# Modulation weights first, probabilities copied in halves, and no scaling of the residual: three edits to one nested two-block transformer kernel

## The chip, the cores and the metric

The kernel runs on one core of a Trainium2 chip. The metric is the device time of one execution, in microseconds (us), as the median of several runs.

## What is computed

Two blocks follow each other on 256 tokens of width 1024, all in 32-bit floats. The first block has two layers, the second has one and a mixture of experts. Cut to what matters here:

```python
# first block: x (256 x 1024) and a context ctx (256 x 1024), two layers i = 0, 1
shift, scale, gate = split(silu(c) @ w_ada[i] + b_ada[i], 3)          # the "modulation"
u, uc = h * (1 + scale) + shift, hc * (1 + scale_c) + shift_c
y, yc = mixer_a(u, uc, ...) if i == 0 else mixer_b(u, uc, ...)        # attention with a gate, 16 heads of 64
h  = layer_norm(ALPHA * h  + gate   * y,  ln_g[i], ln_b[i])           # ALPHA = 4 ** 0.25
hc = layer_norm(ALPHA * hc + gate_c * yc, ln_g[i], ln_b[i])           # only after layer 0
# layer_norm divides by sqrt(var + 1e-5)
# second block, on the 256 rows of h: modulation, dilated attention beside a depthwise
# convolution of width 31, then 32 experts of hidden width 512, two for each token
```

Layer norm doesn't change when its input is divided by a constant, if its 1e-5 is divided by the square of that constant.

## The kernel before, in words

Activations are held turned: features on the 128 partitions, tokens along the free dimension. `H` holds the residual as 8 tiles of 128 x 512 (256 tokens of x, 256 of ctx). Each engine has its own program; semaphores order them.

**Weights.** All weights of the three layers come as chunks of 1024 x 512 (2 MB, 2048 KB in the profile) through `ring`, which has six slots (`SLOTS`). `PLAN` (line 111) fixes their order: four chunks of `ada0` (the modulation of layer 0), three of `a_in`, two more of `ada0`, and so on. SyncE issues them (lines 367 to 379); from the seventh on it waits until the slot's last user is done. Ahead of that loop it issues a table (`cst`), the rows of x and ctx (lines 364, 365), and then line 366 waits for all small vectors. Behind chunk 4 (the first of `a_in`) it issues two constant tables (lines 378, 379).

**The prologue.** ScalarE's queue issues 13 small loads of vectors, the taps of the convolution (`conv_w`) and the sinks (lines 841 to 849). TensorE waits for all of them but the sinks, turns them (lines 472 to 477), then turns the rows of x and ctx, 32 transposes of 128 x 128 in eight groups, which VectorE copies to `H` (line 1081). Then `modulation` (line 507) goes through the four chunks: `stream` (line 486) multiplies a chunk by silu(c) as soon as it has landed, ScalarE copies the row to SBUF (line 861), and `fold` (line 498) turns it into columns. VectorE makes `mod` from them (lines 1100, 1090) and the modulated input `uT` (lines 1105, 1107). TensorE waits for the two tables (line 552) and then runs `in_proj` of `a_in` (line 539), 22 jobs that leave through four PSUM banks.

**Attention.** `attention` stands three times: L = "a" (16 units with 4 key tiles, called lat, then 16 with 2, called ctx), "b" (16 units with 4 key tiles), "c" (8 units with 1 or 2). A unit is two heads of 128 queries. TensorE, for unit n: turns the probabilities of n (line 593), computes the scores of n + 3 (line 583), waits until ScalarE has copied the turned probabilities to `probT` (line 911, one instruction for all key tiles), multiplies them by the values (line 603). ScalarE, after the copy of n, makes the exponentials of n + 2 (line 896, for "a" also line 900 for the sink). VectorE, in its turn n: takes the output of n - 1 (line 1186 or 1188), adds mask or bias to the scores of n + 3 and reduces them to a maximum (lines 1210 or 1221, 1151 to 1156), then divides the exponentials of n + 2 by their sum (lines 1173, 1177).

**The residual.** After `a_in`, ScalarE multiplies all of `H` by ALPHA in place, eight instructions (line 884), before the first exponential of attention "a". VectorE multiplies `ln_g` and `ln_b` of layer 0 by ALPHA (lines 1279, 1280), so that the output of the first layer norm is scaled too. `residual` (line 1239) waits for both by `alpha_ok` and adds gate * y to `H`.

**The experts.** SyncE loads 96 tensors of 2 MB, six for each of 16 pairs of experts. Its waits for free slots are counts of TensorE's, VectorE's and ScalarE's events (lines 393 to 415).

## Time and profile before

| | |
|---|---|
| Median of 3 runs | 1337.2 us (1336.38 to 1338.01) |
| The profiled execution | 1337.21 us, its span 1335.4 us |
| TensorE, matmuls busy | 1245.6 us (93%) |
| VectorE, ScalarE busy | 403.1 us (30%), 293.8 us (22%) |
| Data moved | 310.74 MB, mean 233 GB/s |
| Mean granted clock of TensorE | 0.963 of full |

The profiled execution is one more run than the three, and its time agrees with their median. 1.8 us of it lie outside the span. TensorE is busy nearly everywhere, but not in the first 46 us, and in the last third the data engines run at their peak of about 428 GB/s.

### The profile page before, as it was taken

How to read it: one execution, taken by the hardware profiler on the slowest of the kernel's cores; microseconds unless marked ns; L12 is line 12 of the kernel's file. 1: busy time of each engine (PE TensorE's matmuls, PEld its weight loads, DVE VectorE, ACT ScalarE, POOL GpSimd, SP SyncE). 2: the span in 40 equal slices, each digit the busy share in tenths (PEclk: the TensorE clock that was granted, in tenths of full speed). 3: DMA queues.
4: the chain of work that ended last, by engine and by line, in shares of the span. 5: the costliest groups of instructions: out<-in, count | busy, mean ns of one | idle time of the engine just before them, and what ended most of it. 6: DMA issues, size and time to landing. Idle time of an engine off the chain costs nothing.

```text
span 1335.4 us, 14792 instructions
## 1 busy us (share of the span) xinstructions
PE 1245.6 (93%) x6028; PEld 702.5 (53%) x6028; DVE 403.1 (30%) x966; ACT 293.8 (22%) x627; POOL 18.7 (1%) x27
## 2 busy tenths in 40 slices
PE   4899998999989999899999898899999999999995
PEld 2346445654465446666778468544445544444443
DVE  1212008851230000491319932212112221211223
ACT  0000018860140001471220332111111111111113
POOL 0000000000001000120000000000000000000000
PEclk9899998999989999999889888899999999999998
DMA  8931521025234131527614746579999999999980
GB/s 300 389 113 64 189 87 40 1 81 214 93 132 135 63 124 65 150 48 259 250 64 172 269 189 252 204 300 382 425 429 428 428 429 427 429 427 429 428 364 33
DMA packets 80778, 310.74 MB, mean 233 GB/s; under 512 B 17872, under 2 KB 18203, under 8 KB 68440
## 3 DMA queue, kind: packets, MB, share of 16 engines
q1 hardware_dynamic: 77792, 309.56, 59.2%
q8 instruction: 35, 0.57, 0.2%
q10 hardware_dynamic: 2856, 0.33, 0.2%
q0 software_dynamic: 80, 0.15, 0.0%
q14 instruction: 15, 0.12, 0.0%
HBM read 308.86 MB, written 1.17 MB: 232 GB/s over the span
## 4 chain that ended last, share of the span: by engine, by line
PE 71%; DMA 18%; ACT 5%; DVE 3%; SPq 2%; issue 1%; ACTq 0%; DVEq 0%
PE ps L539 22%; DMA ring<-in_w_exp_up 16%; PE ps L772 12%; PE ps L639 8%; PE ps L535 6%; PE ps L603 4%; PE ps L593 3%; PE ps L799 3%; PE ps L494 3%; ACT probT L911 3%; PE ps L657 3%; PE ps L745 2%; PE ps L754 2%; DMA cst<-in_consts 1%; PE ps L503 1%; SPq L376 1%
## 5 line engine op out<-in xcount | busy, mean ns | idle before, releaser
L539 PE MATMUL ps<-U,ring 128*128 128x256 f32 (+1 forms) x928 | 300.4, 486 | 11.1 <-ACT U L937 4.4
L539 PEld LDWEIGHTS ps<-U,ring 128*128 128x128 f32 x928 | 179.6, 195 | 125.1 <-issue 103.7
L772 PE MATMUL ps<-ring,prob 128*64 128x512 f32 x976 | 217.8, 593 | 6.0 <-DMA ring<-in_w_exp_up 5.2
L772 PEld LDWEIGHTS ps<-ring,prob 128*64 128x64 f32 x976 | 71.5, 137 | 144.4 <-issue 131.4
L799 PE MATMUL ps<-ring,prob 128*64 128x512 f32 x512 | 113.4, 595 | 0.0
L639 PE MATMUL ps<-U,ring 128*128 128x256 f32 (+1 forms) x384 | 110.9, 451 | 0.0
L639 PEld LDWEIGHTS ps<-U,ring 128*128 128x128 f32 x384 | 72.7, 190 | 36.6 <-issue 30.1
L535 PE MATMUL ps<-ring,U 128*128 128x512 f32 (+1 forms) x224 | 83.1, 531 | 0.0
L1482 DVE TENSOR_TENSOR prob<-ps,prob 128x512 f32<-128x512 f32 x16 | 17.2, 1075 | 203.2 <-PE ps L772 203.2
L799 PEld LDWEIGHTS ps<-ring,prob 128*64 128x64 f32 x512 | 35.4, 137 | 66.6 <-issue 66.6
L745 PEld LDWEIGHTS ps<-bias,U 128*128 128x128 f32 x512 | 61.2, 199 | 13.7 <-issue 13.7
L745 PE MATMUL ps<-bias,U 128*128 128x128 f32 x512 | 64.2, 286 | 1.4 <-DVE bias L1449 1.4
L896 ACT ACTIVATE prob<-ps,soft 128x512 f32<-128x512 f32 (+2 forms) x112 | 63.8, 585 | 5.3 <-DVE soft L1156 5.2
L535 PEld LDWEIGHTS ps<-ring,U 128*128 128x128 f32 x224 | 42.6, 190 | 39.5 <-issue 37.8
L494 PE MATMUL ps<-ring,sil 128*32 128x512 f32 x384 | 49.3, 646 | 10.3 <-DMA ring<-in_w_ada 9.6
L754 PE MATMUL ps<-bias,probT 128*128 128x256 f32 x256 | 58.0, 379 | 0.8 <-ACT probT L1028 0.8
L583 PE MATMUL ps<-K,Q 64*128 64x512 f32 (+1 forms) x192 | 47.8, 579 | 9.6 <-ACT soft L900 5.2
L593 PE MATMUL ps<-cst,prob 128*128 128x128 f32 x344 | 53.0, 293 | 2.5 <-DVE prob L1177 2.4
L911 ACT ACTIVATE probT<-ps 128x1024 f32<-128x1024 f32 (+2 forms) x56 | 46.3, 826 | 39.5 <-PE ps L593 38.7
L754 PEld LDWEIGHTS ps<-bias,probT 128*128 128x128 f32 x256 | 47.4, 190 | 7.5 <-ACT probT L1028 1.7
L1470 DVE TENSOR_TENSOR U<-ps,U 128x512 f32<-128x512 f32 x64 | 44.2, 691 | 19.7 <-PE ps L754 19.7
L1347 DVE SCALAR_TENSOR_TENSOR G<-G,conv_taps 128x256 f32<-128x256 f32 x120 | 47.6, 478 | 0.0
(197 smaller groups left out, 928.8 us busy)
## 6 DMA issues: line engine op xcount, KB each, us to landing
ring<-in_w_exp_down SPq DMA_DIRECT2D x32, 2048.0 KB, 12.2
ring<-in_w_exp_up SPq DMA_DIRECT2D x31, 2048.0 KB, 17.3
ring<-in_w_exp_gate SPq DMA_DIRECT2D x30, 2048.0 KB, 15.3
ring<-in_w_ada SPq DMA_DIRECT2D x12, 2048.0 KB, 13.0
ring<-in_w_mod SPq DMA_DIRECT2D x12, 2048.0 KB, 8.2
ring<-in_b_w_in SPq DMA_DIRECT2D x8, 2048.0 KB, 8.4
ring<-in_a_w_in SPq DMA_DIRECT2D x5, 2048.0 KB, 19.8
ring<-in_w_in SPq DMA_DIRECT2D x5, 2048.0 KB, 7.9
```

Source lines behind the costliest of these rows:

```text
L494: last = mm(ps[32 * t:32 * t + 32, bank, :], sil[:, k, :], slot(n)[:, k, :], start=(i == 0), stop=(i == 1))
L535: last = mm(ps[:, b, 0:wid], src[:, k, t * P:(t + 1) * P], w[:, col:col + wid], start=(k == 0), stop=(k == KT - 1))
L539: last = mm(ps[:, b, 0:wid], w[:, col:col + P], src[:, k, 0:wid], start=(k == 0), stop=(k == KT - 1))
L593: last = tr(ps[:, 4 + i // 2, (i % 2) * S + x * P:(i % 2) * S + (x + 1) * P], prob[:, n % AHEAD, x * T + i * P:x * T + (i + 1) * P], ident)
L603: last = mm(ps[x * HD:(x + 1) * HD, 6 + n % 2, 0:P], v_of(2 * p + x, kt), probT[:, i * S + x * P:i * S + (x + 1) * P], start=(i == 0), sto ...
L639: last = mm(ps[:, m % 4, 0:width], slot(n)[:, k, (m % 4) * P:(m % 4 + 1) * P], src[:, k, 0:width], start=(k == 0), stop=(k == KT - 1))
L745: last = mm(ps[:, j // 4, (j % 4) * P:(j % 4 + 1) * P], h2rows[:, t, j * P:(j + 1) * P], pick[:, t, :], start=(t == 0), stop=(t == 1))
L754: last = mm(ps[:, (7, 2, 3, 0)[m // 2], (m % 2) * S:(m % 2 + 1) * S], yrows[:, m * P:(m + 1) * P], wpickT, start=True, stop=True)
L772: last = mm(ps[x * CAP:(x + 1) * CAP, 2 + i, :], xg[:, k, x * CAP:(x + 1) * CAP], chunk(n, 2 * i + x)[0][:, k, :], start=(k == 0), stop=(k ...
L799: last = mm(ps[x * CAP:(x + 1) * CAP, 5 + c, :], hidT[:, k, x * CAP:(x + 1) * CAP], chunk(n, 4 + x)[0][:, k, c * 512:(c + 1) * 512], start ...
L896: last = a(prob[:, n % AHEAD, x * T:x * T + w], ps[:, 2 * (n % 2) + x, 0:w], ACT.Exp, bias=s[:, 1, x:x + 1], accum_out=None if L == "c" el ...
L911: a(probT[:, 0:kts * S], src, ACT.Copy).then_inc(at[L, "copied"], 1)
```

## The change

Three edits:

1. **Order of the prologue.** SyncE no longer waits for the vectors before the first chunk. It issues chunk 0 of `ada0`, the rows of x, chunk 1, the rows of ctx, chunks 2 and 3, and the rest as before. TensorE waits for the vectors without the taps, and turns the rows of x between `stream` of chunk 0 and of chunk 1, the rows of ctx and the taps between chunk 1 and chunk 2, as 16 groups of two transposes. VectorE copies 16 tiles of 128 x 256 for 8 of 128 x 512. The wait for the tables moves behind the second job of `a_in`.
2. **Probabilities in halves.** ScalarE copies the turned probabilities in pieces of two key tiles (128 x 512), and TensorE's multiplication by the values waits for each piece by itself. Units with at most two key tiles are copied in one piece, as before.
3. **No ALPHA.** `H` isn't scaled. The gates are divided by ALPHA instead (one more instruction in `take_gates`, with a wait ahead of it), and the 1e-5 by ALPHA squared. The eight instructions on ScalarE and the two small ones on VectorE go. `residual` of layer 1 waits for the output of the first layer norm.

Beside them, the semaphore `sums` is replaced by the step counter of VectorE.

```diff
@@ SyncE
-            sp.dma_start(xrows[:, 0:2, :], IN["x"][0].rearrange("(t p) f -> p t f", p=P)).then_inc(x_in, 16)
-            sp.dma_start(xrows[:, 2:4, :], IN["ctx"][0].rearrange("(t p) f -> p t f", p=P)).then_inc(x_in, 16)
-            sp.wait_ge(vec_in, 16 * (len(VEC) + 1))
             for n, (stage, src, l, c) in enumerate(PLAN):
...
                 sp.dma_start(slot(n), w).then_inc(full[n % SLOTS], 16)
+                if n in (0, 1):
+                    rows = IN[("x", "ctx")[n]][0].rearrange("(t p) f -> p t f", p=P)
+                    sp.dma_start(xrows[:, 2 * n:2 * n + 2, :], rows).then_inc(x_in[n], 16)
@@ TensorE
-            pe.wait_ge(vec_in, 16 * (len(VEC) + 1))
+            pe.wait_ge(vec_in, 16 * len(VEC))
...
+            def turn_rows(half):
+
+                pe.wait_ge(x_in[half], 16)
+                for j in range(KT):
+                    i = half * KT + j
+                    if i >= 4:
+                        pe.wait_ge(x_ok, i - 3)
+                    for t in range(2):
+                        last = tr(ps[:, 1 + j % 4, t * P:(t + 1) * P], xrows[:, 2 * half + t, j * P:(j + 1) * P], ident)
+                    last.then_inc(pe_x, 1)
...
-            modulation("ada0", range(4), 0, 2, (5, 6), 7)
+            stream("ada0", 0, 5)
+            turn_rows(0)
+            stream("ada0", 1, 6)
+            fold("ada0", 0, 0, 2, 7)
+            turn_rows(1)
+            turn_taps()
+            stream("ada0", 2, 5)
+            fold("ada0", 1, 0, 2, 7)
+            stream("ada0", 3, 6)
+            fold("ada0", 2, 0, 2, 7)
+            fold("ada0", 3, 0, 2, 7)
...
-            pe.wait_ge(table_in, 32)
-
...
                 if 1 <= i <= 10:
                     r = i - 1
+                    if r == 0:
+                        pe.wait_ge(table_in, 32)
...
+            pe.wait_ge(taps_ok, 1)
             in_proj("a_in", uT, {"q": T, "k": T, "g": T}, beside)
...
-                    pe.wait_ge(at[L, "copied"], n + 1)
...
                     for i, kt in enumerate(kts):
+                        if i % 2 == 0:
+                            pe.wait_ge(at[L, "copied"], halves(un, n) + i // 2 + 1)
@@ ScalarE
-            for j in range(KT):
-                act.wait_ge(u_ok, j + 1)
-                a(H[:, j, :], H[:, j, :], ACT.Copy, scale=ALPHA).then_inc(alpha_ok, 1)
...
-                    a(probT[:, 0:kts * S], src, ACT.Copy).then_inc(at[L, "copied"], 1)
+                    for i in range(0, kts, 2):
+                        w = min(2, kts - i) * S
+                        a(probT[:, i * S:i * S + w], ps[:, 4 + i // 2, 0:w], ACT.Copy).then_inc(at[L, "copied"], 1)
@@ VectorE
-            for j in range(KT):
-                dve.wait_ge(pe_x, j + 1)
-                v.tensor_copy(H[:, j, :], ps[:, 1 + j % 4, :]).then_inc(x_ok, 1)
+            for i in range(2 * KT):
+                half, j = i // KT, i % KT
+                dve.wait_ge(pe_x, i + 1)
+                v.tensor_copy(H[:, j, half * S:(half + 1) * S], ps[:, 1 + j % 4, 0:S]).then_inc(x_ok, 1)
...
-                take_columns(l, 16, 24).then_inc(mod_ok, 1)
+                step(take_columns(l, 16, 24))
+                settle()
+                v.tensor_scalar(mod[:, l, 16:24, :], mod[:, l, 16:24, :], 1.0 / ALPHA, None, ALU.mult).then_inc(mod_ok, 1)
...
-            step(v.tensor_scalar(g0, g0, ALPHA, None, ALU.mult))
-            step(v.tensor_scalar(b0, b0, ALPHA, None, ALU.mult))
-            settle()
```

## Rows read from the trace of the kernel before

**Rows 1.** The page: the span.

```profile
span 1335.4 us, 14792 instructions
```

**Rows 2.** The chain that ended last, 0 to 140 us: start us, us, what.

```profile
6.00 6.19 DMA K<-in_conv_w
...
31.04 15.32 DMA cst<-in_consts
...
46.40 16.51 PE ps L539 x32
...
63.34 6.87 PE ps L539 x16
```

**Rows 3.** Timeline of the prologue: start us, us, engine, line, what [idle before].

```profile
1.22 0.42 SPq L364 DMA_DIRECT2D Q<-in_x  x1
...
12.20 9.66 SPq L376 DMA_DIRECT2D ring<-in_w_ada  x4
...
13.55 5.54 PE L483 MATMUL ps<-cst,Q 128*128 128x128 f32 x32
...
15.64 0.23 ACT L854 ACTIVATE sil<-vec 128x24 f32<-128x24 f32 x1
...
25.70 1.92 PE L494 MATMUL ps<-ring,sil 128*32 128x512 f32 x16 [3.41 <-DMA ring<-in_w_ada]
...
38.04 3.48 PE L494 MATMUL ps<-ring,sil 128*32 128x512 f32 x16 [2.40 <-DMA ring<-in_w_ada]
...
43.44 0.19 DVE L1100 TENSOR_TENSOR mod<-ps,vec 128x32 f32<-128x32 f32 x1 [23.09 <-PE ps L503]
...
44.20 0.41 DVE L1107 TENSOR_SCALAR U<-H,mod 128x256 f32<-128x256 f32 x1
```

**Rows 4.** Busy time by stretch: PE, PEld, DVE, ACT, POOL, clock, DMA share, GB/s.

```profile
31.00:38.00 7.00, 4.52 (x24) 1.56 (x24) 0.00 (x0) 0.60 (x1) 0.00 (x0) 0.74 1.05 388
```

**Rows 5.** Timeline between `a_in` and attention "a".

```profile
196.99 4.25 ACT L884 ACTIVATE H<-H 128x512 f32<-128x512 f32 x8
...
200.20 0.16 DVE L1153 TENSOR_TENSOR soft<-soft,negsink 128x2 f32<-128x2 f32 x1
...
201.26 1.28 ACT L896 ACT_TABLE_LOAD   x1
```

**Rows 6.** Timeline of attention "a", units with four key tiles.

```profile
212.56 0.28 DVE L1186 TENSOR_TENSOR U<-ps,G 128x128 f32<-128x128 f32 x1
...
215.74 0.28 DVE L1186 TENSOR_TENSOR U<-ps,G 128x128 f32<-128x128 f32 x1
...
220.24 1.09 PE L593 MATMUL ps<-cst,prob 128*128 128x128 f32 x8
...
221.26 1.13 PE L583 MATMUL ps<-K,Q 64*128 64x512 f32 x4
...
221.37 1.03 ACT L911 ACTIVATE probT<-ps 128x1024 f32<-128x1024 f32 x1 [0.51 <-PE ps L593]
...
222.44 1.09 PE L603 MATMUL ps<-probT,K 128*64 128x128 f32 x16
...
223.47 1.09 PE L593 MATMUL ps<-cst,prob 128*128 128x128 f32 x8
```

**Rows 7.** Timeline of attention "a", units with two key tiles.

```profile
259.73 0.60 ACT L911 ACTIVATE probT<-ps 128x512 f32<-128x512 f32 x1 [0.50 <-PE ps L593]
...
261.66 0.60 ACT L911 ACTIVATE probT<-ps 128x512 f32<-128x512 f32 x1
```

**Rows 8.** Timeline of the last units of attention "b".

```profile
599.11 0.88 DVE L1177 TENSOR_SCALAR prob<-prob,soft 128x512 f32<-128x512 f32 x2
...
600.88 1.09 PE L593 MATMUL ps<-cst,prob 128*128 128x128 f32 x8
...
603.09 1.09 PE L603 MATMUL ps<-probT,G 128*64 128x128 f32 x16 [1.11 <-ACT probT L911]
```

**Rows 9.** Busy time by stretch, as in rows 4: the pairs of experts.

```profile
1000.00:1290.00 290.00, 284.84 (x1486) 138.40 (x1484) 59.37 (x89) 39.27 (x59) 0.00 (x0) 1.00 1.01 428
```

More of the change, by code:

```diff
@@ L96, in constants @@
     put("fold", np.arange(P)[:, None] % 32 == np.arange(3)[None, :])
-    put("eps", np.tile(np.array([1e-5, 1e-6]), (P, 1)))
+    put("eps", np.tile(np.array([1e-5 / ALPHA ** 2, 1e-6]), (P, 1)))
     return out
@@ L171, with halves @@
 AHEAD = 3
+def halves(un, n):
+    return sum(-(-len(u[3]) // 2) for u in un[:n])
 def build(nc, IN, consts_dram, relpad, out):
@@ L288, in build @@
         for L in "abc":
-            for n in ("scores", "max", "exp", "sums", "prob", "turned", "copied", "pv", "o"):
+            for n in ("scores", "max", "exp", "prob", "turned", "copied", "pv", "o"):
                 at[L, n] = sem(f"{L}_{n}")
@@ L470, in _, with turn_taps @@
             pe.wait_ge(cst_in, 16)
[L471 removed]
+            pe.wait_ge(vec_in, 16 * len(VEC))
             tr(ps[:, 0, 0:P], vrows[:, 0, :], ident)
[L473 to L484 removed]
+            tr(ps[:, 0, P:P + VROWS1], vrows[0:VROWS1, 1, :], ident[0:VROWS1, 0:VROWS1]).then_inc(pe_vec, 1)
+            def turn_taps():
+                pe.wait_ge(taps_in, 16)
+                pe.wait_ge(vec_ok, 1)
+                for c in range(4):
+                    last = tr(ps[:, 0, 256 + 32 * c:256 + 32 * c + CONV_W], crows[:, c * P:(c + 1) * P],
+                              ident[0:CONV_W, 0:CONV_W])
+                last.then_inc(pe_vec, 1)
+            def turn_rows(half):
[7 more added lines that the diff above has]
+                    last.then_inc(pe_x, 1)
             def stream(stage, c, bank):
@@ L906, in attention @@
                     kts = len(un[n][3])
-                    src = ps[:, 4, 0:kts * S] if kts <= 2 else ps[:, 4:6, :]
                     act.wait_ge(at[L, "turned"], n + 1)
@@ L1110, in _ @@
             take_modulation(0)
-            dve.wait_ge(x_ok, KT)
+            dve.wait_ge(x_ok, 2 * KT)
             modulate(0)
@@ L1237, in _, with residual @@
             attention("a", mask_a)
-            def residual(stage, l, parts, base):
+            def residual(stage, l, parts):
                 dve.wait_ge(mod_ok, 2 * l + 2)
@@ L1243, in residual @@
                     dve.wait_ge(st[stage], m + 1)
-                    dve.wait_ge(alpha_ok, base + m + 1)
+                    if l == 1:
+                        dve.wait_ge(nm["lna", "out"], m + 1)
                     for i, (c0, c1) in enumerate(parts):
@@ L1278, in _ @@
             settle()
-            step(v.tensor_scalar(g0, g0, ALPHA, None, ALU.mult))
-            step(v.tensor_scalar(b0, b0, ALPHA, None, ALU.mult))
-            settle()
-            residual("a_out", 0, ((0, S), (S, T)), 0)
+            residual("a_out", 0, ((0, S), (S, T)))
             center("lna", T)
@@ L1289, in _ @@
                 v.tensor_scalar(H[:, j, 0:S], H[:, j, 0:S], vc("ln_g", j), vc("ln_b", j), ALU.mult, ALU.add
-                                ).then_inc(alpha_ok, 1)
+                                ).then_inc(nm["lna", "out"], 1)
             take_gates(1)
@@ L1314, in _ @@
             gains(0, "g_norm1_2", 8)
-            residual("b_out", 1, ((0, S),), KT)
+            residual("b_out", 1, ((0, S),))
             center("lnb", S)
```

30 lines of the change are left out of this document (10 added, 20 removed).

## The prediction

> **What bounds the kernel now.** I read four views, in this order. First the page: a span of 1335.4 us [rows 1], beside a profiled execution of 1337.21 us, so 1.8 us lie outside. That execution agrees with the median, 1337.2 us, so what I take off its span comes off the median too. Then the chain that ended last, in order of time: the places that the diff touches can only pay where they stand on it. Then the timeline at each such place, and last the stretches of the experts.
>
> The chain begins with the vectors: the last, `conv_w`, is issued at 6.00 us and lands 6.19 us later [rows 2]. Only then, at 12.20 us, does SyncE issue the first modulation chunk [rows 3]. From there the data engines set the pace: 388 GB/s, a chunk of 2.1 MB every 5.4 us [rows 4]. The reader should see that the fourth chunk's `stream` starts at 38.04 us after idling for it [rows 3], that VectorE has the modulation from 43.44 us on and the first modulated tile at 44.20 + 0.41 = 44.6 us, and that TensorE still stands until 46.40 us, because line 552 wants the tables [rows 2, 3]. After that TensorE works without a gap: jobs of 6.87 us [rows 2].
>
> In attention the unit is a loop. In "a", TensorE turns probabilities at 220.24, computes scores at 221.26, multiplies by values at 222.44, and begins again at 223.47 [rows 6]: 3.23 us. Of this the transposes issue for 1.02, the multiplication by values for 1.03. The scores are four passes of 512 columns; `stream` of the fast kind has 16 such passes, four at a time, in 1.92 us [rows 3], so a pass is near 0.21 us (also 16 of them in 6.87 / 2 = 3.4 us [rows 2]) and four occupy 0.86 us, their row's 1.13 us including the way through the array. That is 2.91 us of work. The missing 0.32 us is the wait for the copy, which ends at 221.37 + 1.03 = 222.40, 0.04 before the multiplication starts [rows 6]. So in these units the copy is on the loop, by 0.32 us, though no view names it as a long wait.
>
> In the experts from 1000 us on the data engines are full: 1.01 of their time, 428 GB/s [rows 9].
>
> **Edit 1, the order of the prologue.** Before, four chunks issued from 12.20 us let the fourth be used at 38.04 [rows 3]: 25.84 us. Now SyncE starts when it issued x before, at 1.22 us [rows 3], and x and ctx (2.1 MB at 388 GB/s: 5.4 us) go ahead of the third and fourth. So the fourth is used at 1.2 + 25.8 + 5.4 = 32.5 us, 5.5 us sooner. The way from there to VectorE's modulation was 43.44 - 38.04 = 5.4 us, to the first tile 1.2 us more [rows 3]. That part has the same operations, so the input is ready at 39.1 us. Is the weight there? The first chunk of `a_in` is 2.1 MB behind, at 32.5 + 5.4 = 37.9 us. Yes, by 1.2 us. The tables come 1.2 MB, some 3 us, later, and TensorE now wants them two jobs after it starts, 13.7 us or more: hidden. If they were late, ropes would wait, not the jobs. TensorE starts `a_in` at 39.1 for 46.4 us: **7.3 us** less, of which 5.5 are the weights and 1.8 the tables.
>
> Can compute keep up? Let V be when the vectors have landed. The transposes of vectors and the table load with silu took from 12.3 to 15.9 [rows 3], less the taps' share of 0.8: 2.8 us. Then TensorE has four `stream`, 1.92 us each (3.48 at the lower clock), the rows of x and ctx (6.8 us before, from 13.55 to the next operation; VectorE's 16 short copies are about as long as the 8 long ones), four `fold` of 1 us and the taps, 0.6 us: 19 us. With the 1.2 us at the end the input is ready at V + 23. It reaches 39.1 if V is 16 us. The last vector without the taps is issued just before 6.00; at the 6.19 us of `conv_w` V is 12. So weights, not vectors, set the end, with 4 us in hand. What hides the moved transposes is the wait for chunks 1 to 3; without it they cost 7 us.
>
> Here a rule of the Trainium skill speaks against the change. The row shows 6.19 us for a small load while at most 2.1 MB were on their way [rows 2]; now ten or more are. The page "DMA: Bandwidth & Descriptors", section "Queues, rings and completion order", says that each data engine takes turns between queues packet by packet, but that a completion is written only after all earlier writes of that engine, across its queues. By the first half of that rule V stays near 12 us and the sum stands; by the second V grows with what is ahead, which is rival C below. No row of before has a small load of another queue under a full stream.
>
> The clock: `stream` took 1.92 us at 25.70 and 3.48 at 38.04, with a granted clock of 0.74 in that stretch [rows 3, 4], and the first two jobs of `a_in` took 16.51 us for twice 6.87 [rows 2]: 2.8 us lost at the lower of the two levels. TensorE will be better fed before 32 us than it was, yet should again wait some us for the fourth chunk. I take no gain; both ends are 0 and 1.6 + 2.8 = 4.4 us, of which the weight's own landing at 37.9 leaves about 1.2 + 2.8 = 4.
>
> **Edit 3, no ALPHA.** ScalarE's eight instructions end at 196.99 + 4.25 = 201.24, and the table load for the exponential starts at 201.26 [rows 5]. Without them it would start when the first maximum is ready, 200.20 + 0.16 = 200.36 [rows 5]: so of 4.25 us only **0.85 us** come out, since what is late next is VectorE's maximum. The two small instructions on VectorE lie beside the out projection of TensorE: nothing. The added one in `take_gates` runs, for layer 0, some 50 us before its user, and for layer 1 beside the projection of "b", where VectorE copies only some jobs: nothing, and 0.4 us each if uncovered. The new wait in `residual` is for work done a whole attention before.
>
> **Edit 2, copies in halves.** A half is a copy of 128 x 512, 0.60 us for 1.03 [rows 6, 7]. The first half has landed 0.64 us after the copies' start, before the scores are through (0.75 us), and the second while the first is multiplied. ScalarE pays at most 2 x 0.60 - 1.03 = 0.17 us a unit, and has 0.51 idle there [rows 6]. So TensorE could run at 2.91 us a unit. But VectorE's own turn lasts 215.74 - 212.56 = 3.18 us [rows 6]; it becomes the bound. TensorE first uses up its lag: VectorE has unit n's probabilities when it begins the next turn (215.74, 218.9), TensorE takes them 1.2 us later (217.0, 220.24). So "a" gives 1.2 us once, 0.05 us for each of some 11 units (0.55), and about 0.3 us for each of the last two, in which VectorE has less to do: 2.3 us. The units of ctx are untouched: one piece, and 261.66 - 259.73 = 1.93 us each by ScalarE without an idle gap [rows 7], so they start 2.3 us earlier and keep it. **2.3 us.**
>
> In "b" VectorE never waits before its last units: it finishes unit 14's probabilities at 599.11 + 0.88 = 599.99, and TensorE turns them at 600.88 [rows 8]. 0.85 us is there to take, and then two units without scores, in which the whole copy stood open (1.11 us idle, rows 8): 0.4 us each, as the second half ends 0.4 us before a whole copy would have let the multiplication reach it. **1.6 us.** If VectorE's pace costs nothing of it, 16 x 0.32 = 5 us in each of "a" and "b" would be the upper end; the lower is nothing in both. Attention "c" has one or two key tiles: nothing.
>
> **The sum.** 7.3 + 0.85 + 2.3 + 1.6 = 12.0 us. Does it reach the end? In the stream of experts the engines are full [rows 9], but each load of the first pairs waits for an event of the compute engines, all of which come 12 us sooner, so the stream moves as a block. 1335.4 - 12.0 + 1.8 = 1325.2 us.
>
> **The rivals.**
>
> B, the clock stays up. For it: TensorE works more evenly before 32 us, and the loss before was real, 16.51 us for 13.74. Against: the wait of some 3 us for the fourth chunk stays, and at such a wait (2.40 us at 38.04, rows 3) the lower level held. It gives 2 to 4 us more: 1322.
>
> C, the vectors are late. For it: nothing like the stream stood beside them before, and in the stream's own queue a table took 15.32 us to land [rows 2]. At 6.0 + 15.3 = 21.3 us for V the input is ready at 44.3 us: 2.1 in place of 7.3, 1330.4. Against: that row is of one queue, in order; the vectors have another.
>
> D, the halves bring nothing, because an exponential or a maximum is late in each unit, or the extra instruction costs ScalarE what it saves TensorE. Then 8.15 us are left: 1329. For it: ScalarE is within 0.5 us of the loop. Against: the 1.2 us in which finished probabilities wait.
>
> E, the other side: the vectors land only behind the whole of what was issued before them. V would be the fourth chunk's time, 32 us; TensorE would start at 55, 8.6 us later than before, and with the 4.75 of the other edits the kernel takes 1341 us. It decides from V = 46.4 + 4.75 - 23 = 28 us on. Against: the taps landed at 12.19 while x and ctx shared the engines.
>
> F, the expert stream takes it all back: 1337. It would need loads whose start doesn't move. The waits of lines 393 to 412 speak against it.
>
> **How the numbers follow.** Forecast 0.60, B 0.14, C 0.12, D 0.08, E 0.02, F and anything else without gain 0.02, and 0.02 for more gain from the halves than I count. The predicted time is that of the first. The range takes in B and D and the better part of C: 1320.5 to 1330.5; the forecast's own is 1323 to 1328. A change below 0.2% (2.7 us) can't be told from none: faster 0.96, same 0.02, slower 0.02.
>
> **What would show it.** In the changed profile: `stream` of the fourth chunk at 32 to 33 us; line 539's successor starting near 39, released by VectorE's input and not by a table; the vectors' release near 12; the table load of the exponential right behind VectorE's first maximum, some 4 us after the last job; units of 3.18 us in "a", released by VectorE's probabilities rather than ScalarE's copy; the chain of the experts unchanged in length. The prediction is wrong if V is beyond 16 us, if the fourth chunk lands later than 34, or if the units still take 3.23.

## The result and the profile after

The changed kernel takes 1324.6 us (median of four executions, 1324.0 to 1327.4) where the kernel before, in the same comparison, takes 1336.85 us (four executions, 1336.4 to 1338.0): a ratio of 0.991, with a 95% interval of 0.989 to 0.993. That is 12.3 us less; the forecast was 12.0 less, 1325.2. The profiled execution of the changed kernel is one of 1324.02 us, so against the profiled one of before the difference to be explained is 13.2 us. Two executions that lie far outside all others, one of the kernel before (3972.5 us) and one of experiment 3 (1666.4 us), are left out of every comparison.

The span, from the page of the changed kernel:

```profile
span 1322.2 us, 14819 instructions
```

The chain that ended last, in order of time (start us, us, what), which answers to [rows 2]:

```profile
11.73 22.91 DMA ring<-in_w_ada
...
41.50 15.67 PE ps L564 x32
...
191.49 1.14 PE ps L609 x4
...
280.21 3.57 PE ps L509 x32
...
594.97 3.57 PE ps L509 x32
```

No constant and no vector is left on the chain: it goes from the ring's chunk to TensorE. The timeline of the prologue, which answers to [rows 3]:

```profile
12.26 0.45 PE L478 MATMUL ps<-cst,K 128*128 128x128 f32 x1 [12.26 <-DMA K<-in_conv_ln_b]
...
34.69 3.55 PE L509 MATMUL ps<-ring,sil 128*32 128x512 f32 x16 [2.47 <-DMA ring<-in_w_ada]
...
38.17 1.97 PE L518 MATMUL ps<-cst,prob 128*128 128x2 f32 x16
...
41.50 15.67 PE L564 MATMUL ps<-U,ring 128*128 128x512 f32 x32 [1.35 <-DVE U L1136]
```

The vectors are there at 12.26 us, as before, under a full stream. The fourth chunk's `stream` (line 509 now) starts at 34.69 us, not at 32.5, and runs at the lower of the clock's two levels, 3.55 us for 1.92. `a_in` then starts at 41.50, 4.9 us sooner than in [rows 2], released by VectorE's modulated tile.

The start of attention "a", timeline, which answers to [rows 5]:

```profile
191.37 1.28 ACT L920 ACT_TABLE_LOAD   x1
...
194.46 0.16 DVE L1182 TENSOR_TENSOR soft<-soft,negsink 128x2 f32<-128x2 f32 x1
...
194.65 0.69 ACT L920 ACTIVATE prob<-ps,soft 128x512 f32<-128x512 f32 x1 [2.00 <-DVE soft L1182]
...
196.52 1.13 PE L609 MATMUL ps<-K,Q 64*128 64x512 f32 x4 [3.04 <-ACT soft L924]
```

The reader should see that the table load starts 3.1 us ahead of the maximum at 194.46 and ends 1.8 us ahead of it: it is off the path altogether.

Units with four key tiles, first in "a" (where [rows 6] showed 3.23 us), timeline:

```profile
207.15 1.09 PE L619 MATMUL ps<-cst,prob 128*128 128x128 f32 x8
...
208.28 1.08 ACT L936 ACTIVATE probT<-ps 128x512 f32<-128x512 f32 x2 [0.32 <-PE ps L619]
...
210.26 1.09 PE L619 MATMUL ps<-cst,prob 128*128 128x128 f32 x8
...
242.00 1.09 PE L619 MATMUL ps<-cst,prob 128*128 128x128 f32 x8 [0.22 <-DVE prob L1206]
```

and in "b", the same view:

```profile
545.83 1.09 PE L619 MATMUL ps<-cst,prob 128*128 128x128 f32 x8 [0.31 <-DVE prob L1206]
546.85 1.13 PE L609 MATMUL ps<-K,Q 64*128 64x512 f32 x4
...
547.91 1.09 PE L630 MATMUL ps<-probT,G 128*64 128x128 f32 x16
548.93 1.09 PE L619 MATMUL ps<-cst,prob 128*128 128x128 f32 x8
```

A unit is now 548.93 - 545.83 = 3.10 us, and the three pieces touch: 1.02 for the transposes, 1.06 for the scores, 1.02 for the values. Two halves take ScalarE 1.08 us, hardly more than the whole copy's 1.03 [rows 6], and it has 0.32 us to spare. Later in "a" TensorE waits a little for VectorE's probabilities (0.22 us at 242.00), and the unit is 3.18 us.

Units with two key tiles, timeline, which answers to [rows 7]:

```profile
254.55 0.60 ACT L936 ACTIVATE probT<-ps 128x512 f32<-128x512 f32 x1
...
256.57 0.60 ACT L936 ACTIVATE probT<-ps 128x512 f32<-128x512 f32 x1
```

The copies are 2.02 us apart, where before they were 1.93. The copy is one piece in both kernels, so the forecast had these units unchanged; here 0.09 us a unit was lost.

Put together, start times of the same work in the two profiled executions:

| work | before | after | gained so far |
|---|---|---|---|
| `stream` of the fourth chunk | 38.04 | 34.69 | 3.35 |
| first job of `a_in` | 46.40 | 41.50 | 4.90 |
| third job of `a_in` | 63.34 | 57.60 | 5.74 |
| first scores of "a" | 197.24 | 191.49 | 5.75 |
| first exponential of "a" | 202.55 | 194.65 | 7.90 |
| `stream` behind "a" | 290.00 | 280.21 | 9.79 |
| first scores of "b" | 549.45 | 539.66 | 9.79 |
| `stream` behind "b" | 607.41 | 594.97 | 12.44 |
| the experts, line 799 now | 848.31 | 835.19 | 13.12 |
| end of the span | 1335.4 | 1322.2 | 13.2 |

Most of it is gained at places that the diff touches, and what is gained is kept to the end. Two steps lie elsewhere: 0.84 us between the first and the third job of `a_in`, and 0.68 us between the `stream` behind "b" and the experts. Both kernels do the same work there, and what differs in the traces is the granted clock.

### The profile page after: what moved, and what is told of

It is laid out like the page before. It is cut to its first block, busy times and chain, and to the rows that moved or that the text cites. A ratio compares the mean times of both kernels' runs of the same rounds, so it can differ in the third digit from the quotient of the medians.

```text
span 1322.2 us, 14819 instructions
## 1 busy us (share of the span) xinstructions
PE 1237.7 (94%) x6028; PEld 697.4 (53%) x6028; DVE 402.6 (30%) x974; ACT 292.0 (22%) x651; POOL 18.7 (1%) x27
## 4 chain that ended last, share of the span: by engine, by line
PE 70%; DMA 18%; DVE 7%; ACT 3%; SPq 1%; issue 1%; DVEq 0%
PE ps L564 22%; DMA ring<-in_w_exp_up 16%; PE ps L799 12%; PE ps L666 8%; PE ps L560 6%; PE ps L826 3%; PE ps L509 3%; PE ps L684 3%; PE ps L630 2%; PE ps L619 2%; PE ps L772 2%; PE ps L609 2%; DMA ring<-in_w_ada 2%; PE ps L781 2%; DVE soft L1180 1%; DVE prob L1206 1%
## 5 line engine op out<-in xcount | busy, mean ns | idle before, releaser
L936 ACT ACTIVATE probT<-ps 128x512 f32<-128x512 f32 (+1 forms) x88 | 48.2, 585 | 33.0 <-PE ps L619 30.8
```

The lines of the kernel that those rows point to most:

```text
L936: a(probT[:, i * S:i * S + w], ps[:, 4 + i // 2, 0:w], ACT.Copy).then_inc(at[L, "copied"], 1)
```

## The experiments

Four questions: what each edit is worth alone (1 to 3), why the units with two key tiles grew longer (4), why the fourth chunk came at 34.7 and not at 32.5 (6, 7), and what TensorE's clock costs in the prologue and in attention (5, 8, 9 to 12). The kernel before takes 1337.5 us beside experiments 1 to 4, 1336.7 beside 5 to 8, and 1335.9 beside 9 to 12 (medians). Where fillers are added, they are matrix multiplications whose result nothing reads.

### 1. The order of the prologue alone

The changed kernel with edits 2 and 3 undone:

```
-                    for i in range(0, kts, 2):
-                        w = min(2, kts - i) * S
-                        a(probT[:, i * S:i * S + w], ps[:, 4 + i // 2, 0:w], ACT.Copy).then_inc(at[L, "copied"], 1)
+                    src = ps[:, 4, 0:kts * S] if kts <= 2 else ps[:, 4:6, :]
+                    a(probT[:, 0:kts * S], src, ACT.Copy).then_inc(at[L, "copied"], 1)
...
+            for j in range(KT):
+                act.wait_ge(u_ok, j + 1)
+                a(H[:, j, :], H[:, j, :], ACT.Copy, scale=ALPHA).then_inc(alpha_ok, 1)
```

> Edit 1 alone: the new order of the prologue, with whole copies and with the scaling by ALPHA as before. Theory 1 (what the two traces show): the projection of a_in starts at 41.5 us for 46.4 and its third job at 57.6 for 63.3, and nothing else moves, so the time falls by 5.7 us, to about 1331. The prediction's own term was 7.3 us. Theory 2: a part of the 13 us between the two profiled executions came of the prologue in another way (a better clock later on), then 6.5 us or more are gained here. The idle time of TensorE ahead of the first exponentials, 5.2 us, should be unchanged, since ALPHA is still applied.

Measured: 1331.1 us, ratio 0.9955 (0.994 to 0.997): 6.0 us. Its timeline:

```profile
34.68 3.64 PE L509 MATMUL ps<-ring,sil 128*32 128x512 f32 x16 [0.70 <-DMA ring<-in_w_ada]
38.25 3.58 PE L518 MATMUL ps<-cst,prob 128*128 128x2 f32 x16
...
43.18 15.94 PE L564 MATMUL ps<-U,ring 128*128 128x512 f32 x32 [1.36 <-DVE U L1135]
```

The fourth chunk is used at 34.68 us again, so its time belongs to the order of the loads. But here the folds too run at the lower level (3.58 us for 1.97 in the changed kernel), and `a_in` starts 1.7 us later than there, with the same work ahead of it. What the clock does in the prologue differs from execution to execution. By the chain of this trace the third job starts at 59.55 us, so this execution, of 1332.65 us one of the longer ones of its five, had gained 3.8 us by then and not 5.7.

### 2. The halves alone

The kernel before with edit 2:

```
+                        if i % 2 == 0:
+                            pe.wait_ge(at[L, "copied"], halves(un, n) + i // 2 + 1)
...
+                    for i in range(0, kts, 2):
+                        w = min(2, kts - i) * S
+                        a(probT[:, i * S:i * S + w], ps[:, 4 + i // 2, 0:w], ACT.Copy).then_inc(at[L, "copied"], 1)
```

> Edit 2 alone: probabilities copied in halves, all else as before. Theory 1: attention a gains 1.7 us in its units with four key tiles and loses 1.4 in those with two, whose period goes from 1.93 to 2.02 us; attention b gains 2.6 us; together 2.9 us, to about 1334. Theory 2: the longer period of the units with two key tiles is an effect of another edit (another phase of the engines after the removed scaling); then it stays 1.93 here and the gain is 4.3 us. The prediction had 3.9 us, by 2.3 and 1.6.

Measured: 1334.0 us, ratio 0.9974 (0.9964 to 0.9984): 3.5 us. In its trace "b" is 2.5 us shorter than in the kernel before (units of 3.11 us), and "a" 0.9, from the first exponential to the `stream` behind it. The units with two key tiles are as long as in the changed kernel, 258.41 - 256.39 = 2.02 us by its timeline:

```profile
256.39 0.60 ACT L918 ACTIVATE probT<-ps 128x512 f32<-128x512 f32 x1
...
258.41 0.60 ACT L918 ACTIVATE probT<-ps 128x512 f32<-128x512 f32 x1
```

So the halves' own code makes them longer, and not the other two edits.

### 3. The scaling of the residual alone

The kernel before with edit 3:

```
-            for j in range(KT):
-                act.wait_ge(u_ok, j + 1)
-                a(H[:, j, :], H[:, j, :], ACT.Copy, scale=ALPHA).then_inc(alpha_ok, 1)
```

> Edit 3 alone: no scaling by ALPHA, all else as before. Prediction's term: 0.85 us. Theory 1: the table load of the exponential no longer comes behind the first maximum but is through before it, so the first exponential starts 2.15 us sooner, and since TensorE then stands only about 3 us and not 5.2, its next operations run at the upper of its two clock levels, which gives about 1.6 us more: 3.7 us, to about 1333. Theory 2: the clock has to do with other edits, and the gain is 2.1 us.

Measured: 1334.4 us, ratio 0.9974 (0.9963 to 0.9984): 3.5 us, four times the forecast's 0.85. Its timeline, in an execution that at 1339.0 us is the longest of the ten that are compared:

```profile
197.16 1.28 ACT L893 ACT_TABLE_LOAD   x1
...
200.44 0.69 ACT L893 ACTIVATE prob<-ps,soft 128x512 f32<-128x512 f32 x1 [2.00 <-DVE soft L1152]
...
202.31 2.08 PE L583 MATMUL ps<-K,Q 64*128 64x512 f32 x4 [3.04 <-ACT soft L897]
```

The table load has moved ahead of the maximum, and the first exponential comes 202.55 - 200.44 = 2.11 us sooner than before. That is shown. But the next scores, behind the same 3.04 us of idle time as in the changed kernel, take 2.08 us here and took 1.13 there: the same stand leaves TensorE at the lower level in one execution and at the upper in another. It stood 5.20 us at this place in the kernel before, and was at the lower level after it. This execution as a whole gained nothing (a span of 1337.1 us for 1335.4): its first units ran longer than those of the kernel before, from one set of transposes to the next 5.15 us for 4.10 in "a" and 4.11 for 3.24 in "b". Of the 3.5 us by which the ten executions are shorter on average, 2.1 are the table load's; the rest goes with the clock as far as these traces tell, and is argued, not isolated.

### 4. The two waits in the other order

TensorE waits ahead of the values for the copy and for a free output bank ("o"). Edit 2 turned their order round; this experiment is the changed kernel with the old order:

```
+                    pe.wait_ge(at[L, "copied"], halves(un, n) + 1)
                     if n >= 2:
                         pe.wait_ge(at[L, "o"], n - 1)
                     for i, kt in enumerate(kts):
-                        if i % 2 == 0:
-                            pe.wait_ge(at[L, "copied"], halves(un, n) + i // 2 + 1)
+                        if i == 2:
+                            pe.wait_ge(at[L, "copied"], halves(un, n) + 2)
```

> The kernel with all three edits, but TensorE waits first for the (first) copy and then for VectorE's output buffer, as the kernel before had it; the second half is waited for behind the first multiplications. Theory 1: the order of these two waits made the units with two key tiles 0.09 us longer (2.02 for 1.93 us); put back, attention a ends 1.4 us sooner and the time is about 1323.1 for 1324.6. Theory 2: the period has another cause, such as the phase in which the engines enter these units, and stays 2.02; the time is the same within 0.3 us.

Measured: 1323.4 us, ratio 0.9901 (0.9886 to 0.9916). Its timeline in the units with two key tiles:

```profile
249.99 0.60 ACT L937 ACTIVATE probT<-ps 128x512 f32<-128x512 f32 x1
...
250.64 0.66 PE L631 MATMUL ps<-probT,K 128*64 128x128 f32 x8
...
251.92 0.60 ACT L937 ACTIVATE probT<-ps 128x512 f32<-128x512 f32 x1
```

1.93 us again, to the hundredth, and the multiplication by the values starts 0.05 us after the copy's end at 250.59. In the changed kernel it started 0.14 us after the end at 257.17, by its timeline:

```profile
257.31 0.66 PE L630 MATMUL ps<-probT,K 128*64 128x128 f32 x8
```

That settles it: the order of two waits on one engine is worth 0.09 us a unit, 16 units, 1.4 us. The medians of the two kernels can't show it (the same file, timed again as experiment 12, gave 1325.1); the period in the trace does, in every trace with either order.

### 5. Long fillers in the prologue

On top of experiment 4: 4, 5 and 2 fillers of 512 columns, ahead of the third `stream`, ahead of the fourth, and behind the last `fold`.

```
+            pe.wait_ge(x_ok, 2 * KT)
+            fill(4, 1, xrows[:, 0, 0:512])
             stream("ada0", 2, 5)
             fold("ada0", 1, 0, 2, 7)
+            fill(5, 1, xrows[:, 0, 0:512])
...
             fold("ada0", 3, 0, 2, 7)
+            fill(2, 1, xrows[:, 0, 0:512])
```

> e4 with eleven matmuls of 128 x 512 that serve nothing (their result is never read), in the three stretches of the prologue in which TensorE stood: four before the stream of chunk 2, five before that of chunk 3, two before a_in. Theory 1: TensorE's lower clock around 35 to 46 us comes of those stretches. Fed, the stream of chunk 3 takes 1.92 us for 3.43, and the first two jobs of a_in 13.7 us for 15.6, so the third job of a_in starts up to 3.4 us earlier than at 57.24, unless the weights of a_in, which land somewhere before 41.2, stop it: 1 to 3.4 us less, 1320 to 1322.4. Theory 2: the clock falls all the same, and the time is that of e4, or up to 1 us more where a filler delays a stream.

Measured: 1325.9 us, ratio 0.9918 (0.990 to 0.9936). Timeline:

```profile
33.54 4.54 PE L531 MATMUL ps<-Q,cst 128*128 128x512 f32 x10
38.01 1.92 PE L509 MATMUL ps<-ring,sil 128*32 128x512 f32 x16
...
43.47 13.90 PE L573 MATMUL ps<-U,ring 128*128 128x512 f32 x32
```

The five fillers are ten instructions and take 4.54 us, twice what I had meant, so they hold the fourth `stream` until 38.01, 3.3 us late. Behind them it takes 1.92 us, and the first two jobs 13.90: the upper level, as expected. What the late start costs and what the clock gives cancel.

### 6. The taps in two loads

On top of experiment 4, the 31 rows of `conv_w` are loaded as 16 and 15:

```
-            act.dma_start(crows, IN["conv_w_2"][0]).then_inc(taps_in, 16)
+            act.dma_start(crows[0:16], IN["conv_w_2"][0][0:16]).then_inc(taps_in, 16)
+            act.dma_start(crows[16:CONV_W], IN["conv_w_2"][0][16:CONV_W]).then_inc(taps_in, 16)
```

> e4 with the taps of the convolution loaded as 16 and 15 rows for 31 rows at once. The Trainium skill, page DMA: Bandwidth & Descriptors, section Why a DMA increments its semaphore by 16 and not by 1, says that a load is spread over the largest number of data engines up to 16 that divides its rows, so 31 rows come through one engine. The expectation itself: the fourth chunk was used at 34.6 us where the sum of bytes gave 32.5. Theory 1: one engine is held up by the 62 KB of the taps and its share of the chunks is late; in two pieces the chunk is used 1 us or more earlier and the time falls by as much, to about 1322. Theory 2: the chunk is late for the bytes of everything ahead of it and a slower start of the stream; it is used at 34.6 as before and the time stays 1323.4 within 0.5.

Measured: 1324.7 us, ratio 0.9917 (0.990 to 0.9934). Timeline:

```profile
27.35 1.93 PE L509 MATMUL ps<-ring,sil 128*32 128x512 f32 x16 [1.18 <-DMA ring<-in_w_ada]
...
33.39 3.64 PE L509 MATMUL ps<-ring,sil 128*32 128x512 f32 x16 [3.14 <-DMA ring<-in_w_ada]
36.96 3.58 PE L518 MATMUL ps<-cst,prob 128*128 128x2 f32 x16
...
41.89 15.62 PE L564 MATMUL ps<-U,ring 128*128 128x512 f32 x32 [1.35 <-DVE U L1138]
```

The third chunk is used 1.8 us sooner than in experiment 4 (29.16), the fourth 1.2 us sooner (34.56). In experiments 10 and 11, which load the taps in the same way, the fourth chunk is used at 33.86 and 33.78 us, 0.6 to 0.9 us sooner than in experiments 4, 9 and 12 (34.56, 34.48, 34.63). So a load of 62 KB did hold up a stream of chunks of 2 MB, by 0.6 to 1.2 us: a quarter to a half of the 2.2 us by which the fourth chunk missed the forecast. It held up what was behind it in its own queue too: the sinks (8 KB) landed 11.8 us after their issue in experiment 4 and 6.8 us after it here. The page "DMA: Bandwidth & Descriptors" of the Trainium skill, section "Why a DMA increments its semaphore by 16 and not by 1", says that the number of engines which share a load has to divide its outermost dimension, and so is one for 31 rows. The traces agree as far as they go: both delays shrink when the rows are 16 and 15; how many engines carried the load no view here shows. The time doesn't fall: behind a longer stand (3.14 us) the fourth `stream` and the folds are at the lower level, and `a_in` starts later than in experiment 4 (41.22).

### 7. ctx behind the last chunk

On top of experiment 4, the rows of ctx are issued behind the fourth chunk and transposed behind the folds:

```
-                if n in (0, 1):
-                    rows = IN[("x", "ctx")[n]][0].rearrange("(t p) f -> p t f", p=P)
+                if n in (0, 3):
+                    i = n // 3
+                    rows = IN[("x", "ctx")[i]][0].rearrange("(t p) f -> p t f", p=P)
...
             fold("ada0", 3, 0, 2, 7)
+            turn_rows(1)
```

> e4 with the rows of ctx loaded behind chunk 3 for between chunks 1 and 2, and turned after the last fold. Theory 1: bytes ahead of the fourth chunk set its time, so it is used 2.7 us sooner, at about 31.9; a_in then starts at 39.6 to 40.3 for 41.2, held by the copies of ctx or by its own weights, 1 to 1.5 us less: about 1322.2. Theory 2: the weights of a_in, whose place in the order is unchanged, are what lands last anyway; a_in starts at 41 and nothing is gained. Theory 3: the transposes of ctx, no longer hidden, come on the path for their whole 2.4 us and it gets slower by 1 us.

Measured: 1325.9 us (four executions from 1322.3 to 1328.8), ratio 0.9925 (0.9897 to 0.9953). Timeline:

```profile
32.11 3.54 PE L510 MATMUL ps<-ring,sil 128*32 128x512 f32 x16 [2.50 <-DMA ring<-in_w_ada]
...
37.38 2.96 PE L499 MATMUL ps<-cst,Q 128*128 128x128 f32 x16
...
41.72 15.92 PE L565 MATMUL ps<-U,ring 128*128 128x512 f32 x32 [1.38 <-DVE U L1141]
```

The chunk comes 2.45 us sooner, close to what the 1 MB of ctx takes at 388 GB/s (2.7 us), and the 2.96 us of transposes, which the wait for chunks hid before, now stand open. In this execution `a_in` starts at 41.72 us, for 41.22 in experiment 4 and 43.14 in experiment 12: the sooner chunk brought nothing, since work moved out of a wait has to be paid. That this order is worse than the diff's the times don't show; the two intervals overlap.

### 8. Long fillers in attention

On top of experiment 4, six fillers of 512 columns ahead of the third unit's scores in "a" and "b":

```
                 for n in range(AHEAD):
+                    if n == 2 and L in "ab":
+                        for _ in range(6):
+                            mm(ps[:, 7, :], ident, uT[:, 0, :], start=True, stop=True)
                     scores(n)
```

> e4 with six matmuls of 128 x 512 that serve nothing between the second and the third scores at the start of attention a and of b, where TensorE stood for 3.0 and 2.7 us. Theory 1: such a stand brings the lower clock in some executions (the first scores after it took 1.13 us in one profile and 2.08 in another, and the first unit 3.1 or 4.3 us); fed, they never do, so the median falls by up to 1 us and the scatter gets smaller, 1322.4 to 1323.4. Theory 2: the clock after it doesn't depend on these few us, and the time is that of e4 or up to 0.5 us more, since six matmuls of 0.43 us fill 2.6 us and may delay the scores.

Measured: 1326.2 us, ratio 0.992 (0.9904 to 0.9937). Timeline:

```profile
193.36 5.42 PE L616 MATMUL ps<-U,cst 128*128 128x512 f32 x12
```

5.42 us of fillers where TensorE stood 3.04: they overrun by 2.4 us, and from the first scores of "a" to the `stream` behind it 89.4 us go by, for 87.1 in experiment 4. On what the clock costs there this run says nothing.

### 9. Short fillers in the prologue

Experiment 5 with 256 columns and 3, 4 and 3 of them:

```
+                    mm(ps[:, bank, 0:256], ident, src, start=True, stop=True)
...
+            fill(3, 1, xrows[:, 0, 0:256])
             stream("ada0", 2, 5)
             fold("ada0", 1, 0, 2, 7)
+            fill(4, 1, xrows[:, 0, 0:256])
...
+            fill(3, 1, xrows[:, 0, 0:256])
```

> e5 again with fillers that fit: matmuls of 128 x 256 (0.43 us each, by e5's rows for 512 columns), three before the stream of chunk 2, four before that of chunk 3, three before a_in. In e5 the fillers were twice as long as meant and held the stream of chunk 3 back to 38.0 us, while the clock stayed at the upper level. Theory 1: now the stream of chunk 3 starts at 34.6 as in e4 and takes 1.92 us, a_in starts at 39.8 to 40.3 for 41.2 and its first two jobs take 13.7 for 15.6; the third job starts at 54.1 to 54.5 for 57.1, and the time is 2.5 to 3 us below e12's. Theory 2: with less filling the clock falls as in e4, and nothing is gained.

Measured: 1320.3 us, ratio 0.989 (0.9873 to 0.9907). Timeline:

```profile
34.48 1.92 PE L509 MATMUL ps<-ring,sil 128*32 128x512 f32 x16 [0.64 <-DMA ring<-in_w_ada]
...
39.92 13.97 PE L573 MATMUL ps<-U,ring 128*128 128x512 f32 x32 [0.24 <-DMA ring<-in_a_w_in]
```

The chunk comes when it came before, 34.48 us; everything behind it runs at the upper level. `a_in` now waits 0.24 us for its own weight, which bounds what is left here.

### 10. Short fillers and the taps in two

Experiment 6's loads, with no filler ahead of the third `stream`, six ahead of the fourth and four at the end.

> e6 (taps in two loads) with six such fillers before the stream of chunk 3 and four before a_in. In e6 the chunks were used at 27.4 and 33.4 us for 29.2 and 34.6, but the wait before the fourth became 3.1 us and the two folds after it ran at the lower clock, so a_in started no earlier. Theory 1: the 1.2 us were given back by the clock; fed, they come out beside e9's gain, a_in starts at 39 and its third job at 53.3, and the time is 3.5 to 4 us below e12's. Theory 2: the weights of a_in land only at 40 us or later and hold a_in; then e10 is no better than e9.

Measured: 1320.4 us, ratio 0.9886 (0.9869 to 0.9902). Timeline:

```profile
33.86 1.92 PE L509 MATMUL ps<-ring,sil 128*32 128x512 f32 x16 [1.06 <-DMA ring<-in_w_ada]
...
39.33 13.97 PE L572 MATMUL ps<-U,ring 128*128 128x512 f32 x32
```

Both are 0.6 us sooner than in experiment 9, which the medians don't resolve.

### 11. Attention too

Experiment 10 and five fillers of 256 columns ahead of the third unit's scores in "a" and "b":

```
+                    if n == 2 and L in "ab":
+                        for _ in range(5):
+                            mm(ps[:, 7, 0:256], ident, uT[:, 0, 0:256], start=True, stop=True)
```

> e10 with five such fillers (2.15 us) between the second and the third scores at the start of attention a and b; in e8 six of twice the length overran the stand of 3.0 and 2.7 us. Theory 1: the lower clock after those stands costs about 1 us where it comes (first unit 4.3 for 3.1 us), so the median falls by up to 1 us against e10 and the scatter gets smaller. Theory 2: no difference from e10 within 0.4 us, as the stands bring the lower clock in few executions.

Measured: 1319.8 us (1318.0 to 1324.0), ratio 0.9878 (0.986 to 0.9897), the lowest median of all: 16 us below the kernel before. Busy time of each engine in the stretch from 190 us (PE, PEld, DVE, ACT, POOL, clock, DMA share, GB/s), first experiment 9, then this one:

```profile
190.00:205.00 15.00, 11.97 (x74) 6.72 (x72) 12.63 (x30) 9.64 (x29) 0.00 (x0) 0.77 0.33 124
```

```profile
190.00:205.00 15.00, 14.13 (x109) 8.82 (x107) 14.26 (x36) 12.64 (x38) 0.00 (x0) 1.00 0.28 106
```

The granted clock is 1.00 for 0.77, and the first two copies come 198.12 - 195.01 = 3.11 us apart, where experiment 9's first unit took 4.18. From the first exponential of "a" to the `stream` behind it this execution takes 84.0 us, those of experiments 9 and 10 take 85.9. Yet the median is only 0.6 us below experiment 10's. From the `stream` behind "b" to the experts, where the two kernels do the same work, this execution takes 241.0 us for 237.7 in experiment 10, and a stretch of the norms there has a granted clock of 0.83 (650 to 670 us) for 1.00 (651.5 to 671.5). The 1.9 us in "a" are shown by the trace, their worth in the time is not. Nor do they need fillers: experiment 4's execution took 84.0 us there as well.

### 12. Experiment 4 again

The same kernel, beside 9 to 11, to have the comparison under the same conditions.

> e4 once more, beside the three kernels that are built on it: 1323.4 us, with its third job of a_in at 57 us and units with two key tiles of 1.93 us.

Measured: 1325.1 us (1321.3 to 1326.2), ratio 0.9908 (0.9893 to 0.9924). Timeline:

```profile
34.63 3.64 PE L509 MATMUL ps<-ring,sil 128*32 128x512 f32 x16 [1.05 <-DMA ring<-in_w_ada]
38.20 3.58 PE L518 MATMUL ps<-cst,prob 128*128 128x2 f32 x16
...
43.14 16.13 PE L564 MATMUL ps<-U,ring 128*128 128x512 f32 x32 [1.36 <-DVE U L1137]
```

One kernel, two executions: here `a_in` starts at 43.14, in experiment 4 at 41.22, and the difference is the folds' clock. In attention "a" they differ once more: behind the same idle time of 3.04 us the next scores took 2.08 us here and 1.13 in experiment 4, and from the first exponential to the `stream` behind "a" it is 85.9 us for 84.0. Against this run the three kernels with short fillers are 4.8, 4.7 and 5.3 us faster by the medians, and 3.0, 3.7 and 4.4 by the means. Their traces have the third job of `a_in` at 54.3, 53.7 and 53.7 us, that is 3 to 6 us ahead of experiments 4 (57.2) and 12 (59.7), and that is the gain, some 3 to 5 us in the time.

## Why the prediction was right, and where its terms were not

**The time.** 12.0 us was forecast and 12.3 measured. The three edits alone take off 6.0, 3.5 and 3.5 us, 13.0 together, and within the 2 to 3 us that these intervals leave that agrees with 12.3: no sign that they get in each other's way. The sum is better than its terms, none of which came as written.

**The order of the prologue: 7.3 forecast, 6.0 measured alone, 5.75 by the trace of the changed kernel (3.8 by that of experiment 1).** The mechanism is as told: vectors at 12.26 us, weights set the end, tables no longer wait. The way from the fourth `stream` to the first modulated tile was put at 6.6 us and took 41.50 - 34.69 = 6.8. The step that failed is "so the fourth is used at 1.2 + 25.8 + 5.4 = 32.5": it was 34.7. By the prediction's own sign ("if the fourth chunk lands later than 34") this step is wrong. Of these 2.2 us, 0.6 to 1.2 are the taps' load (experiments 6, 10 and 11), which in the kernel before was over ahead of the first chunk and now runs beside the chunks. The rest isn't settled. What speaks for the slow start of the queue: between 0 and 5 us the changed kernel moved 167 GB/s, so the bytes that I carried at 388 GB/s from 1.2 us on couldn't move at that rate. The clock then gave 0.85 us back, since the first two jobs took 15.67 for 16.51 us; I had put it at nothing, with an end of 4.

**No ALPHA: 0.85 forecast, 3.5 measured.** The step was "without them it would start when the first maximum is ready": I took the table load to wait with its exponential for VectorE. It doesn't. In the changed kernel it starts when ScalarE is free and is over 1.8 us before the maximum. The kernel before had shown this in "b", where there is no ALPHA; its timeline:

```profile
549.37 1.28 ACT L896 ACT_TABLE_LOAD   x1
549.45 1.99 PE L583 MATMUL ps<-K,Q 64*128 64x512 f32 x8 [0.52 <-issue]
```

The load at 549.37 starts before the scores that the maximum is taken from. I read one of the two places only. So the load's own 1.28 us come off the path as well: 0.85 + 1.28 = 2.13, and the trace has 7.90 - 5.75 = 2.15. Behind it comes the clock, about 1 us in the first unit where it stays up. That was luck: behind the same stand of 3.04 us it stayed up in the executions of the changed kernel and of experiments 4, 6 and 7, and not in those of experiments 3, 5, 9, 10 and 12. Behind 5.2 us (the kernel before, experiments 1 and 2) it didn't stay up in any of three, which is too few to say that the shorter stand helps.

**The halves in "a": 2.3 forecast, 0.9 measured in experiment 2.** The units with four key tiles gave what they should: 3.11 and 3.18 us for 3.23, and shorter last ones. The step that failed is "the units of ctx are untouched". Their copy is; the order of TensorE's two waits isn't, and it cost 16 x 0.09 = 1.4 us. 0.9 + 1.4 = 2.3, of which some 0.2 lie in the first unit (3.74 us for 4.10), where the clock differed. Experiment 4 shows the cause by putting the order back.

**The halves in "b": 1.6 forecast, 2.65 by the trace, 2.5 in experiment 2.** The unit didn't fall to 2.91 us of work and VectorE's 3.18, but to TensorE's own floor, and that is 3.10: the reading that four passes of scores occupy 0.86 us was wrong, since they issue 1.06 apart. So the whole copy had held a unit by 0.12 to 0.13 us and not by 0.32, and the 5 us that the prediction had as its upper end were never there. The step that failed is "0.85 us is there to take". That was VectorE's lead at the end of "b" in the kernel before, and two of its turns there were longer than the others, next to GpSimd's work; timeline of the kernel before:

```profile
563.63 1.50 DVE L1177 TENSOR_SCALAR prob<-prob,soft 128x512 f32<-128x512 f32 x2
563.93 1.91 POOL L449 TENSOR_TENSOR bias<-bias,cst 128x384 f32<-128x384 f32 x2 [3.92 <-DMA bias<-relpad]
```

1.50 us at 563.63 for the usual 0.88 [rows 8], and again 1.46 at 576.71. TensorE kept its 3.23 us through both, so they cost the kernel before nothing; but they used up 1.2 us of the lead that faster units can take. In the changed kernel's "b" no such row is longer than 0.88. 1.6 + 1.2 is 2.8, and 2.65 came. Why the two engines' work fell apart this time, and whether GpSimd's was the cause at all, no experiment isolates. Nor is 2.65 the gain of every execution: from the first scores of "b" to the `stream` behind it the kernel before took 57.9 us and the changed one 55.3, but experiment 4, with the same halves, took 57.6 and its repetition, experiment 12, 55.4. In experiment 4 the scores behind TensorE's stand of 2.73 us ran at the lower level (1.81 us for 1.13) and the first unit took 4.44 us for 3.11.

**The rivals.** B, the clock stays up, happened in part: 0.85 us in the first jobs, about 1 us in the first unit of "a", 0.7 us in the norms behind "b". Experiments 9 to 11 show what the upper level is worth in the prologue, 3 to 6 us by the traces. C and E, late vectors, fell: 6.16 us from the issue of the last vector at 6.10 to its use at 12.26, beside a stream of 370 GB/s. The second half of the rule that the prediction took from the Trainium skill ("DMA: Bandwidth & Descriptors", "Queues, rings and completion order") would have made this row grow with the stream ahead of it; the trace doesn't show that. What did come late, 11.9 us after its issue for 6.1 before, is the load of the sinks behind the taps, which nothing wants before attention, and experiment 6 puts that on the taps (6.8 us). D fell with the period of 3.11 us, F with the table above: the experts' chain is as long as it was.

**The total.** By the trace the terms were off by -1.5 us in the prologue, +1.3 and another 1 by the clock at the start of "a", -1.4 in the halves of "a", +1.0 in "b", and +0.7 in the norms, which makes +1.1 on the forecast's 12.0, for the 13.2 us of the two profiled executions. They cancel for the most part, and that is luck. The last one alone shows how much: from the `stream` behind "b" to the experts the profiled executions of one and the same kernel took 239.1 us (experiment 4) and 237.7 (experiment 12), and that of the changed kernel 240.2. A total that is right to 0.3 us by the medians says nothing about any of them, only the rows at each place do.

## What to carry to other kernels

When a stretch of idle time is filled by reordering loads, look at what else will now run beside them: a load of 62 KB in 31 rows was over before the stream, and cost it 0.6 to 1.2 us when it came to lie beside it. Before putting down a step as "waits for X", look for a second place in the trace where the same instruction stands without the work in question; the table load in "b" was such a place. And where TensorE stood for some 2.5 us at a time in the prologue, a few short multiplications that nothing reads, sized so that they end before the data comes, were worth some 3 to 5 us here; too long ones cost what they brought.

## What the runs showed of the hardware

- The order of two semaphore waits ahead of one multiplication counts. With the wait that comes true last (here the copy) put first, the multiplication started 0.05 us after the copy's end and a unit took 1.93 us; with it put last, 0.14 us and 2.02.
- A table load of ScalarE doesn't wait for the operands of the activation it serves: it ran at 191.37 us for an activation released at 194.46. Here the page "ScalarE: Activation LUTs" of the Trainium skill, section "What ACT_TABLE_LOAD costs", gives 1.28 us for the load, and the trace agrees with 1.28.
- The same idle time of 3.04 us left TensorE at the upper level of its clock in one execution (scores of 1.13 us) and at the lower in another (2.08), and that in one and the same kernel (experiments 4 and 12). In experiments 9 to 11 no idle time of TensorE from the second `stream` to the third job of `a_in` was longer than 1.3 us, and the rows there ran at the upper level.
- A multiplication of 512 fp32 columns by 128 x 128 is two instructions and took 0.91 us (experiment 5); three of 256 columns took 1.56 (experiment 9).
- A load of 62 KB in 31 rows held up a stream of 2 MB chunks in another queue by 0.6 to 1.2 us and a load behind it in its own queue by 5 us (11.8 us to landing for 6.8); as 16 and 15 rows it didn't (experiments 4 and 6).
- A copy of 1024 columns from PSUM took ScalarE 1.03 us, two of 512 took 1.08: cutting it in halves costs 0.05 us.
